# Query norms of a hybrid decoder step: sums of squares from sixteen one-column products, or from four heads at a time on four column tiles

## The reference, cut to what matters

```
h = rmsnorm(x, norm_w) @ w_in              # 320 tokens x 2048: query half, gate half
q, g = split(h)
q = rmsnorm(q.reshape(.., 8 heads, 128), q_norm_w) * 128 ** -0.5
```

## Time and profile before

| | |
|---|---|
| median of 3 executions | 524.47 us (524.45 to 525.76) |
| the profiled execution, its own time | 524.96 us |
| its span, first to last instruction | 523.2 us |
| TensorE busy | 515.1 us (98%) |
| VectorE, ScalarE, GpSimd busy | 342.4 us (65%), 257.7 us (49%), 72.2 us (14%) |
| memory traffic | 125.52 MB, mean 240 GB/s |
| granted TensorE clock | 1.0 throughout |

### The profile page before, as it was taken

One profiled execution on the slowest core, in us unless ns is written; L12 is line 12 of the kernel. 1 busy time (PEld: TensorE's weight loads), 2 busy tenths in 40 slices (PEclk: granted clock), 3 DMA queues, 4 the chain that ended last, 5 costly groups with the idle time before them and its releaser, 6 DMA issues.

```text
span 523.2 us, 9484 instructions
## 1 busy us (share of the span) xinstructions
PE 515.1 (98%) x3595; PEld 445.2 (85%) x3595; DVE 342.4 (65%) x628; ACT 257.7 (49%) x511; POOL 72.2 (14%) x81
## 2 busy tenths in 40 slices
PE   7999999999999999999999999999999999999997
PEld 6889977899779977897899999988887778999886
DVE  2775448892878738892698967645756764776531
ACT  5826442572338532562743455744444655555520
POOL 0291004420091004420000130100000000000000
PEclk9999999999999999999999999999999999999999
DMA  7983979999999999989747966516797557682211
GB/s 223 361 303 133 267 243 344 382 297 229 323 352 322 225 262 321 378 264 212 235 147 274 337 195 230 172 52 241 232 337 242 206 187 242 237 299 105 81 50 51
DMA packets 78865, 125.52 MB, mean 240 GB/s; under 512 B 3859, under 2 KB 41828, under 8 KB 78692
## 3 DMA queue, kind: packets, MB, share of 16 engines
q1 hardware_dynamic: 78738, 124.89, 74.1%
q10 hardware_dynamic: 82, 0.02, 0.0%
HBM read 98.93 MB, written 27.57 MB: 242 GB/s over the span
## 4 chain that ended last, share of the span: by engine, by line
PE 86%; ACT 5%; DVE 5%; DMA 2%; issue 1%; ACTq 0%; SPq 0%; DVEq 0%
PE bank L823 37%; PE bank L820 19%; PE bank L809 7%; PE bank L988 3%; PE bank L934 3%; DVE w_lo L1433 2%; PE bank L1002 2%; ACT w_hi L1118 2%; PE bank L1055 1%; PE bank L952 1%; PE bank L906 1%; DMA w_raw<-in_ret_w_in 1%; PE bank L893 1%; PE bank L835 1%; PE bank L1094 1%
## 5 line engine op out<-in xcount | busy, mean ns | idle before, releaser
L1433 DVE TENSOR_TENSOR w_lo<-w_raw,w_hi 128x512 fp32r<-128x512 f32 x206 | 145.1, 742 | 72.1 <-ACT w_hi L1118 71.8
L1118 ACT ACTIVATE w_hi<-w_raw 128x512 fp32r<-128x512 f32 x208 | 118.6, 620 | 49.4 <-PE bank L823 22.2
L823 PE MATMUL bank<-xn_hi,w_hi 128*128 128x320 f32 x320 | 100.6, 318 | 0.9 <-DVE w_lo L1433 0.5
L823 PE MATMUL bank<-xn_hi,w_lo 128*128 128x320 f32 x320 | 97.6, 309 | 0.0
L823 PE MATMUL bank<-xn_lo,w_hi 128*128 128x320 f32 x320 | 97.5, 309 | 0.0
L820 PE MATMUL bank<-w_hi,xn_hi 128*128 128x512 f32 x160 | 65.6, 410 | 0.0
L823 PEld LDWEIGHTS bank<-xn_hi,w_hi 128*128 128x128 f32 x320 | 59.7, 188 | 4.6 <-issue 2.8
L820 PE MATMUL bank<-w_lo,xn_hi 128*128 128x512 f32 x160 | 62.7, 392 | 0.0
L820 PE MATMUL bank<-w_hi,xn_lo 128*128 128x512 f32 x160 | 62.5, 391 | 0.0
L823 PE MATMUL bank<-ym_hi,w_hi 128*128 128x320 f32 x192 | 61.8, 322 | 0.0
L823 PEld LDWEIGHTS bank<-xn_lo,w_hi 128*128 128x128 f32 x320 | 59.8, 188 | 0.5
(11 more groups left out here) (228 smaller groups left out, 743.9 us busy)
## 6 DMA issues: line engine op xcount, KB each, us to landing
w_raw<-in_ret_w_in SPq DMA_DIRECT2D x23, 1024.0 KB, 10.8
st<-in_state_ret SPq DMA_DIRECT2D x32, 512.0 KB, 8.2
out_ret_state_sample<-st SPq DMA_DIRECT2D x32, 512.0 KB, 4.7
w_raw<-in_ret_w_out SPq DMA_DIRECT2D x8, 1024.0 KB, 9.2
w_raw<-in_moba_w_in SPq DMA_DIRECT2D x8, 1024.0 KB, 6.7
cache<-in_cache_k SPq DMA_DIRECT2D x16, 512.0 KB, 5.2
w_raw<-in_w_kv SPq DMA_DIRECT2D x8, 1024.0 KB, 6.1
cache<-in_cache_v SPq DMA_DIRECT2D x16, 512.0 KB, 4.5
```

Source lines behind the costliest of these rows:

```text
L823: mm = pe.matmul(bank[out][:, 0:T], w[:, wk, P * tile:P * tile + P], x[:, k, :], **flags)
L1118: act.activation(w_hi[:, c % 2, part], w_raw[:, c % RAW, part], ACT.Copy).then_inc(w_hi_done, 1)
L1433: dve.tensor_tensor(w_lo[:, c % 2, part], w_raw[:, c % RAW, part], w_hi[:, c % 2, part].bitcast(F32), ALU.subtract).then_inc(w_lo_done, 1)
```

## The change: what it does

The squares of six heads have buffers now (`sqp(h)`; heads 6 and 7 use those of 0 and 1). The products take the squares as the moving operand, 256 columns for a head, and a mask `pick` as the standing one: 32 columns of a 33-column buffer that is zero but for one column of ones, so that the sum of the squares comes out in row 0 (heads 0 to 3) or row 1 (heads 4 to 7) of a column tile of 32 rows, and zero is added elsewhere. `QS 0` does heads 0 to 3, one on each column tile, behind `ME 5`; `QS 1` does heads 4 to 7 in the place of the old `QS 7`, and then the four sample products as before. `QR` takes the roots of the four sample columns and copies the 256 columns of bank 7 to `q_rows`, a place in `tb`. A new step `QT`, in the middle of the third tile of the key chunk, transposes the two halves of `q_rows` into bank 7; ScalarE takes roots of 8 columns of each, VectorE the reciprocals. `q_sq_done` is raised by the squares of the sample columns (L1184), not by the copy to `mqT`. GpSimd writes `pick` ahead of `wide`.

```diff
-    mid = [[("NS", KT - 1)]] + [[("ME", n)] + ([("QS", n - 2)] if n >= 2 else []) for n in range(MH - 1)]
+    mid = [[("NS", KT - 1)]] + [[("ME", n)] + ([("QS", 0)] if n == 5 else []) for n in range(MH - 1)]
...
-    g[0] += [("ME", 7), ("QS", 5)]
-    g[1].append(("QS", 6))
-    g[2] += [("QS", 7), ("QR",)]
+    g[0].append(("ME", 7))
+    g[2] += [("QS", 1), ("QR",)]
+    g[4].append(("QT",))
...
-                    h = step[1]
-                    pe.wait_ge(q_done, h + 1)
-                    if h == 0:
+                    g = step[1]
+                    pe.wait_ge(q_sq_done, 4 * g + 4)
+                    if g == 0:
+                        pe.wait_ge(wide_cleared, 1)
                         await_free(pe, 7, "QSS")
-                    for t in range(2):
-                        mm = pe.matmul(bank[7][:, 2 * h + t:2 * h + t + 1], sqp[:, h % 2, P * t:P * t + P], ones[:, 0:1],
-                                       start=True, stop=True)
-                    if h < MH - 1:
+                    for j in range(4):
+                        mm = pe.matmul(bank[7][32 * j:32 * j + 32, 0:TP], pick[:, 1 - g:33 - g], sqp(4 * g + j),
+                                       start=g == 0, stop=g == 1)
+                    if g == 0:
                         mm.then_inc(qs_done, 1)
...
+                elif kind == "QT":
+                    await_free(pe, 7, *step)
+                    for t in range(2):
+                        mm = pe.transpose(bank[7][:, P * t:P * t + P], q_rows[:, P * t:P * t + P], ident)
+                    close(mm, 7)
...
-                    if head >= 2:
-                        act.wait_ge(qs_done, head - 1)
-                    act.activation(sqp[:, head % 2, :], ps[:, head % 2, 0:TP], ACT.Square)
-                    act.activation(sqs[:, :, head, :], ps[:, head % 2, TP:T].rearrange("p (g m) -> p g m", g=2), ACT.Square)
+                    if head >= 6:
+                        act.wait_ge(qs_done, 1)
+                    act.activation(sqp(head), ps[:, head % 2, 0:TP], ACT.Square)
+                    act.activation(sqs[:, :, head, :], ps[:, head % 2, TP:T].rearrange("p (g m) -> p g m", g=2), ACT.Square)\
+                        .then_inc(q_sq_done, 1)
...
                 elif kind == "QR":
                     await_full(act, 7, "QSS")
-                    act.activation(rsq[:, :], bank[7][:, 0:20], ACT.Sqrt, bias=eps[:, 1:2]).then_inc(bank_read[7], 1)
+                    act.activation(rsq[:, 16:20], bank[7][:, TP:TP + 4], ACT.Sqrt, bias=eps[:, 1:2])
+                    act.activation(q_rows, bank[7][:, 0:TP], ACT.Copy).then_inc(bank_read[7], 1)
+                elif kind == "QT":
+                    await_full(act, 7, *step)
+                    roots = rsq[:, 0:16].rearrange("p (i j t) -> p t j i", i=2, j=4)
+                    for t in range(2):
+                        ins = act.activation(roots[:, t], bank[7][:, P * t:P * t + P].rearrange("p (j m) -> p j m", m=32)[:, :, 0:2],
+                                             ACT.Sqrt, bias=eps[:, 1:2])
+                    ins.then_inc(bank_read[7], 1)
...
-                    done(dve.reciprocal(rsq[:, :], rsq[:, :]))
+                    done(dve.reciprocal(rsq[:, 16:20], rsq[:, 16:20]))
+                    done.wait()
+                elif kind == "QT":
+                    await_read(dve, 7, *step)
+                    done(dve.reciprocal(rsq[:, 0:16], rsq[:, 0:16]))
                     done.wait()
...
                 elif kind == "MB":
                     await_ret_over(pool)
+                    done(pool.memset(pick[:, :], 0.0))
+                    done.wait()
+                    pool.memset(pick[:, 1:2], 1.0)
                     pool.memset(wide[:, :, :], 0.0).then_inc(wide_cleared, 1)
```

More of the change, by code:

```diff
@@ L392, in build @@
         sqs = flat_ktc[:, 1, 0:4 * P].rearrange("p (g h m) -> p g h m", g=2, m=32)
-        sqp = flat_ktc[:, 1, 4 * P:D].rearrange("p (s t) -> p s t", s=2)
+        q_rows = tb[:, 0, :]
         ops = ps.ap().rearrange("p s t -> p (s t)")[:, 0:4 * P]
@@ L399, in build @@
         knw = mb("knw", [P, HD])
+        pick = mb("pick", [P, 33])
         rsq, nmxs, dens = small[:, 0:20], small[:, 20:24], small[:, 24:28]
@@ L441, in build @@
         wide_cleared, pads_cleared = sem("wide_cleared"), sem("pads_cleared")
-        qs_done = sem("qs_done")
+        qs_done, q_sq_done = sem("qs_done"), sem("q_sq_done")
         cache_loaded = [sem(f"cache_loaded{i}") for i in range(NCP)]
@@ L536, in y_parts, with sqp @@
             return hi[:, k0:k0 + 4, 0:T], lo[:, k0:k0 + 4, :]
+        def sqp(h):
+            s, at = (0, TP * (h % 6)) if h % 6 < 4 else (1, TP * (h % 6 - 2))
+            return flat_ktc[:, s, at:at + TP]
         def up_bank(b, d):
@@ L742, in _ @@
                     if n == 10:
+                        await_full(sp, 7, "QT")
                         sp.dma_start(tb[:, :, :], bass.AP(scratch.tensor, FAR - P, [[skew, P], [LINE, MH], [1, TP]]))\
@@ L977, in _ @@
                         for pair in range(4):
-                            mm = pe.matmul(bank[7][:, 16 + pair:17 + pair], flat_ktc[:, 1, P * pair:P * pair + P], ones[:, 0:1],
+                            mm = pe.matmul(bank[7][:, TP + pair:TP + pair + 1], flat_ktc[:, 1, P * pair:P * pair + P], ones[:, 0:1],
                                            start=True, stop=True)
                         close(mm, 7)
+                elif kind == "QT":
[3 more added lines that the diff above has]
+                    close(mm, 7)
                 elif kind == "KP":
```

## The result

The kernel after took 526.38 us in the median of 20 executions (523.80 to 529.64), the kernel before 524.69 us of 20 (523.43 to 526.14). The ratio is 1.0031, with a 95% interval of 1.0016 to 1.0045: slower by about 0.3%, where 524.1 us and no measurable change had been forecast, and outside the range of 523.3 to 525.4.

The account below looks back on a forecast made before the run. The stage was taken as bound by a loop of VectorE and ScalarE, not TensorE. -0.70 + 0.12 + 0.23 = -0.35 us took the 524.47 us median to 524.1 us, range 523.3 to 525.4.

Parts of the forecast that it names:

- The loop sets the stage and does not move: Up to `mqT` of head 7, VectorE and ScalarE wait for each other in turn; no link is TensorE's, so timing stays.
- QS 1 starts on the squares and not on `mqT`: At the wait for head 7, `QS 1` starts at 345.74 in place of 346.44 us: -0.70 us.
- The prices: TensorE costs of the new work: 0.58 us for each `QS`, 0.23 for `QT`, sample products staying at 0.90.
- Copies and roots of `QR` and `QT` at nothing: Behind `QS 1`, ScalarE's copy and roots and VectorE's reciprocals were expected to delay no TensorE products: 0 us.
- Sum -0.35 us: Whole path: -0.70 at the wait, +0.12 for `QS 1`, +0.23 for `QT`.
- The idle of about 2.2 us ahead of QS 1: TensorE, freed of old `QS` work, would stand still from about 343.5 to 345.74 us, released by ScalarE's squares.
- The clock rival: TensorE's idle ahead of `QS 1` lowers its clock: ten records' worth, 1.9 us, come back, giving 526.0 us; chance 6%.
- the idle of 0.92 us a few microseconds on: TensorE's idle near the program's start in the earlier trace; the transpose records after it were not slow.
- ten slow records at the start: At the program's start, after standing still, ten records of 256 columns take 0.40 us each, against 0.21 later.
- Its own sign of being wrong: Behind TensorE's idle ahead of `QS 1`, records starting twice as far apart would show the forecast wrong.

Follow-up runs that it names:

- e10: Kernel after with VectorE's `ps` moved ahead of both quarters of the weight split, ScalarE's order kept; 522.53 us, ratio to before 0.9956.
- e8: Kernel after with the four sample products 64 columns wide instead of one; 525.94 us, ratio to before 1.0023.
- e1: Kernel after with five unused plain products (ten records) put in front of the wait of `QS 1`; 524.52 us, ratio to before 0.9995.
- e2: Kernel after with two unused plain products put in front of the wait of `QS 1`; 524.85 us, ratio to before 1.0001.
- e4: Kernel before with the twelve products of `QS 0` to `QS 5` left out; 525.83 us, ratio to before 1.0014.
- e3: Kernel after with `QS 1`, `QR`, `KP 0` and `KP 1` one step later, behind six more key-tile products; 522.61 us, ratio to before 0.9961.

## Why the prediction was wrong

Its mechanism was right and its ranking of the rivals was not. Step by step:

- *The loop sets the stage and does not move.* Right: 31.66 against 31.65 us to `ps` of head 7, and e10 shows that the removed products do count once the loop is gone (1.9 us of stage, where its expectation had 2.2: a `QS` amid other products costs 0.76 us).
- *QS 1 starts on the squares and not on `mqT`.* Right: 347.44 against the end of L1196 at 347.39.
- *The prices.* `QS` 0.58 us, measured 0.57 (0.76 amid other products, which nobody waits for here). `QT` 0.23, measured 0.22. Sample products 0.90, measured 0.98: they follow on column tiles now. Copies and roots of `QR` and `QT` at nothing: right, no wait in front of `KP 1` or `QT`. Sum -0.35 us; measured -0.4 in the stage of e8 and -0.44 in the six executions at full clock. e1 gives -0.3 and e8 +0.5 in their times, so the size is borne out by the stage alone, and only roughly.
- *The idle of about 2.2 us ahead of QS 1.* Foreseen, measured 2.02.
- *The clock rival at 6%, worth 1.9 us, and at nothing in the sum.* This is the step that failed. Both halves were read from the earlier trace rows: "the idle of 0.92 us a few microseconds on" was taken as a sign that an idle of 2.2 us would do no harm, and ten slow records at the start as the length of a fall. Its own sign of being wrong, records twice as far apart behind the idle, is what came (16 transposes in 3.52 us, in place of 1.81). In the runs, 0.7 us of standing still never lowered the clock (7 executions), 1.2 us in 2 of 12, 2.0 us in 14 of 20. The long fall holds half rate for 6.8 us (347.9 to 354.7 us in the profile after): transposes 3.52 - 1.81 = 1.71 us, sample products 1.80 - 0.98 = 0.82, six products of the tile 2.05 - 1.39 = 0.66, `QS 1` 0.10; 3.3 us together, with -0.35 the +2.9 us of the stage. The medians with and without the long fall lie 3.9 us apart (528.19 against 524.25); the rows do not account for the other 0.6 us. The price was off by nearly a factor of two or more and, if 14 of 20 is the measure, the chance by more than ten.

The page that the prediction named for this, "TensorE: Matmul & The Clock Gate" of the Trainium skill, Part 1, says that half rate is the default and that activity releases it. The runs agree: the rate fell behind TensorE's standing still, in kernels with and without the change, and did not fall where the wait was filled (0 of 12). A rule with that content should not have been set aside on one idle of less than half the length.

What stays open: why the fall has two lengths (a mean clock of 0.997 goes with 3.4 us at half rate in the profiles of e2 and e4, 0.994 with 6.8 us in that of the kernel after), and why some executions escape it, such as that of e8 with the same wait. e8 hints that the work behind the wait matters for the length, with too few executions to say.

## What to carry to other kernels

Before taking work off an engine that shows 98% busy, look whether the chain of waits runs through it. If the next wait is for a loop of other engines, the work taken out comes back as standing still, and on TensorE that can cost more than the work did: here 2 us of it brought a fall of the clock worth 3.3 us in half of the executions. So move work into the wait (e3) or shorten the loop (e10) in the same edit, and when an order is changed, count how often the work changes hands in a turn, not the instructions.

## What the runs showed of the hardware that was not expected

- A single wait of 2.02 us in a stream that was otherwise full took the granted clock to 0.50 for 6.8 us; 6 of the 20 executions of the same program show a clock of 1.000, and the profile of e8 shows a wait of 2.0 us with no fall behind it. The median of a few executions of such a kernel moves with the luck of the draw: 523.80 to 529.64 us.
- Taking twelve products out made a kernel no faster and probably slower (525.83 against 524.64 us before); putting ten useless records in made one faster (524.52 against 526.38, by the ratios to before 0.9995 against 1.0031).
- A group of products on column tiles cost 0.19 us beyond its own 0.57 where it stands amid plain products, and 0.09 us in one-column products behind it.
